# A decoder step on one core: 32 column diagonal tiles for the recurrence's levels, merged masked copies, and another order in sample attention

## The reference, cut to what matters

```python
rel = exp(b[t] - b[s]) for s <= t            # b: running sum of log f
att[t, s] = sum_k q[t, k] * rel[t, s, k] * k_[s, k]
o = att @ i + (q * exp(b)) @ state
```

```python
score = einsum('bqh,bqhs->bqs', wi, relu(qi . ki_all)) ; top_idx = top_k(score, 64)
logits = q . k_all[top_idx] * scale ; p = softmax(logits) ; o = p @ v_all[top_idx]
```

## Time and profile before

| | us |
|---|---|
| median of 3 runs (2674.17 to 2674.98) | 2674.17 |
| the profiled execution's own time | 2675.92 |
| its span, first to last instruction | 2674.1 |
| PE matmuls busy | 2607.7 |
| DVE, ACT, POOL busy | 915.5, 841.2, 1096.8 |

### The profile page before, as it was taken

One profiled execution on the slowest core, in us unless ns is written; L12 is line 12 of the kernel. 1 busy time (PEld: TensorE's weight loads), 2 busy tenths in 40 slices (PEclk: granted clock), 3 DMA queues, 4 the chain that ended last, 5 costly groups with the idle time before them and its releaser, 6 DMA issues. The chain is left out here.

```text
span 2674.1 us, 55031 instructions
## 1 busy us (share of the span) xinstructions
PE 2607.7 (98%) x22892; PEld 2484.1 (93%) x22892; DVE 915.5 (34%) x2323; ACT 841.2 (31%) x1359; POOL 1096.8 (41%) x886
## 2 busy tenths in 40 slices
PE   6999999999999999999999999999999999999998
PEld 4999998999988989999999999989998889899998
DVE  4111113267793441111131111134678824311111
ACT  2321222323464233222233222233244622331221
POOL 4444345333322454444554344542343326444443
PEclk9999999999999999999999999999999999999999
DMA  6434444312223434332633322641222234222322
GB/s 249 142 127 150 142 161 154 128 64 91 94 65 95 156 106 142 124 106 94 198 131 128 125 97 94 204 157 64 64 91 80 64 95 175 79 91 83 105 81 81
DMA packets 107060, 312.96 MB, mean 117 GB/s; under 512 B 18476, under 2 KB 45130, under 8 KB 89434
## 3 DMA queue, kind: packets, MB, share of 16 engines
q1 hardware_dynamic: 97952, 290.60, 32.0%
q10 hardware_dynamic: 8906, 19.44, 2.0%
HBM read 299.56 MB, written 10.66 MB: 116 GB/s over the span
## 5 line engine op out<-in xcount | busy, mean ns | idle before, releaser
L956 POOL TENSOR_TENSOR w_lo<-raw,w_hi 128x512 fp32r<-128x512 f32 (+1 forms) x800 | 1004.6, 1286 | 1543.1 <-ACT w_hi L1023 1535.3
L2186 PE MATMUL bank<-h_hi,w_hi 128*128 128x260 f32 x3744 | 1064.2, 284 | 2.8 <-ACT silu_g L1070 2.4
L2187 PE MATMUL bank<-h_hi,w_lo 128*128 128x260 f32 x3744 | 1053.0, 281 | 0.0
L2188 PE MATMUL bank<-h_lo,w_hi 128*128 128x260 f32 x3744 | 1052.7, 281 | 0.0
L2186 PEld LDWEIGHTS bank<-h_hi,w_hi 128*128 128x128 f32 x3744 | 702.5, 188 | 26.4 <-issue 23.9
L2187 PEld LDWEIGHTS bank<-h_hi,w_lo 128*128 128x128 f32 x3744 | 702.7, 188 | 0.0
L2188 PEld LDWEIGHTS bank<-h_lo,w_hi 128*128 128x128 f32 x3744 | 702.7, 188 | 0.0
L1023 ACT CAST w_hi<-raw 128x2048 fp32r<-128x2048 f32 (+3 forms) x219 | 376.5, 1719 | 478.6 <-PE bank L2188 375.8
L2186 PE MATMUL bank<-mid_hi,w_hi 128*128 128x260 f32 x1232 | 349.9, 284 | 0.0
L2188 PE MATMUL bank<-mid_lo,w_hi 128*128 128x260 f32 x1232 | 348.7, 283 | 0.0
L2187 PE MATMUL bank<-mid_hi,w_lo 128*128 128x260 f32 x1232 | 348.3, 283 | 0.0
(11 more groups left out here) (346 smaller groups left out, 3267.1 us busy)
## 6 DMA issues: line engine op xcount, KB each, us to landing
raw<-in_w SPq DMA_DIRECT2D x120, 1024.0 KB, 4.8
raw<-in_w SPq DMA_DIRECT2D x64, 512.0 KB, 4.5
raw<-in_w SPq DMA_DIRECT2D x32, 768.0 KB, 4.3
ada_ring<-in_ada SPq DMA_DIRECT2D x82, 256.0 KB, 5.2
raw<-in_w SPq DMA_DIRECT2D x32, 640.0 KB, 4.2
ada_ring<-in_ada SPq DMA_DIRECT2D x57, 320.0 KB, 5.3
ada_ring<-in_ada SPq DMA_DIRECT2D x57, 192.0 KB, 5.1
ada_low<-in_ada SPq DMA_DIRECT2D x20, 256.0 KB, 4.5
```

The source lines that it names most:

```text
L956: last = pool.tensor_tensor(w_lo[j][:, cols], raw[j][:, cols], w_hi[j][:, cols].bitcast(F32), ALU.subtract)
L2186: mm(out, wh(wb), xh(xb), start=(n == 0), stop=False)
L2187: mm(out, wl(wb), xh(xb), start=False, stop=False)
L2188: last = mm(out, wh(wb), xl(xb), start=False, stop=(n == len(blocks) - 1))
```

## The change

- `SAMPLE_FILLS` has ten places for nine. Group 31 goes from the place ahead of the key transposes to the one behind them; group 38 goes between the values and the transpose of the output; group 39 stays behind that transpose. ACT and PE follow the same table.
- DVE makes `own_diag` ahead of the reciprocal. The semaphore is renamed.
- The four masked copies of a level become one instruction over all chunks, with the mask broadcast over them.
- PE computes levels with 2h <= 32 (h = 1 to 16) as 32x32 tiles on the diagonal, four to a chunk. Level 0 stays whole, and 32 and 64 as they were. The rest of the bank isn't written; the masks don't take from it.

```diff
-SAMPLE_FILLS = ((27, 28), (29,), (30, 31), (32,), (33,), (34, 35), (36,), (37,), (38, 39))
+SAMPLE_FILLS = ((27, 28), (29,), (30,), (31, 32), (33,), (34, 35), (36,), (37,), (38,), (39,))
+TILE = 32
...
             # ACT, sample_attention
-                sample_fill(l, 7)
-                sample_fill(l, 8)
+                for place in (7, 8, 9):
+                    sample_fill(l, place)
...
             # DVE, hgrn: scores
-                    for c in range(TT):
-                        last = v.copy_predicated(
-                            att[:, c, :].rearrange("p (m a h) -> p m a h", a=2, h=h)[:, :, 1, :],
-                            masks[n].bitcast(U32),
-                            src[:, c * P:(c + 1) * P].rearrange("p (m a h) -> p m a h", a=2, h=h)[:, :, 1, :])
-                    last.then_inc(done, 1)
+                    v.copy_predicated(
+                        att[:].rearrange("p c (m a h) -> p c m a h", a=2, h=h)[:, :, :, 1, :],
+                        bc(masks[n].bitcast(U32).unsqueeze(1), [P, TT, m, h]),
+                        src[:, :].rearrange("p (c m a h) -> p c m a h", c=TT, a=2, h=h)[:, :, :, 1, :]).then_inc(done, 1)
...
             # DVE, sample_attention
+                v.tensor_scalar(own_diag[:], ident[0:NB * NH, 0:NB * NH], prob_s[:, PAST:LVIS], None, ALU.mult)\
+                 .then_inc(own_diag_ready, 1)
                 link(v.reciprocal(st_s[:, 3:4], st_s[:, 2:3]))
-                v.tensor_scalar(own_diag[:], ident[0:NB * NH, 0:NB * NH], prob_s[:, PAST:LVIS], None, ALU.mult)\
-                 .then_inc(own_scaled_probs, 1)
...
             # PE, hgrn
-                            if n < MASKED:
+                            if n == 0:
                                 last = mm(out[:, cs], hk[hd % 2][:, cs], qt[:, cs], start=True, stop=True)
+                                continue
+                            if 2 * h <= TILE:
+                                for s0 in range(0, P, TILE):
+                                    both = slice(c * P + s0, c * P + s0 + TILE)
+                                    last = mm(out[s0:s0 + TILE, both], hk[hd % 2][:, both], qt[:, both],
+                                              start=True, stop=True)
                                 continue
...
             # PE, sample_attention and merge
                 mm(out[0:NB * NH, 0:P], own_prob[:], vals[0:NB, TT, :], start=False, stop=True).then_inc(side_full, 1)
+                sample_fill(l, 8)
                 out = open_side(l, "s_oT")
...
             def merge(l):
-                sample_fill(l, 8)
+                sample_fill(l, 9)
```

More of the change, by code:

```diff
@@ L640, in build @@
         s_probs_ready = sem("s_probs_ready")
-        own_scaled_probs = sem("own_scaled_probs")
+        own_diag_ready = sem("own_diag_ready")
         blk_ready = sem("blk_ready")
@@ L2780, in sample_attention @@
                                         ident[0:NB * NH, 0:NB * NH])
-                pe.wait_ge(own_scaled_probs, l + 1)
+                pe.wait_ge(own_diag_ready, l + 1)
                 mm(out[0:NB, 2 * NB * NH:3 * NB * NH], gather_heads[:], own_diag[:], start=True, stop=True)\
```

## The result

Timed in turn with the kernel before (five runs each), the changed kernel takes 2660.38 us in the median (2658.65 to 2661.58) against 2674.17: ratio 0.9945, 95% interval 0.9932 to 0.9957. It is faster by 13.8 us between the medians, by 14.7 by the ratio. Forecast were 16.2 us, and 2658.0 us.

What follows compares the result with a forecast made beforehand. PE, busy 98% of the span, was taken as the bound. 12.4 + 0 + 3.0 + 0 + 0.8 = 16.2 us off the median of 2674.17 gave 2658.0 us, own range 2654 to 2662, or 2652 to 2667 with partial overlap and the clock.

Steps and rivals of the forecast that it cites:

- How a level costs PE: PE at the levels: 0.89 us for a wide level, 0.57 for h=32, of which 0.32 is the change of tile shape.
- part 1: Diagonal tiles on PE, h=1 to 16: four strips overlap, each of 40 levels saves 0.31 us, 12.4 us in all.
- The first rival: Levels on PE: tiles overlap only in part, 13.6 ns a start, 40 levels save 5.5 us, time 2664.9; chance 0.13.
- the floor: Rival at the cut levels: about 25 ns from start to start, 0.80 us for 32 starts, time 2679.5; chance 0.04.
- The stop before h=64: PE's stops there in heads 1 and 2: PE and DVE both move by about 0.6 us, so 0 saved.
- Part 2: Merged masked copies on DVE: 7 us of DVE time less over 40 levels, hidden from PE, so costed at nothing.
- Part 3: Key transposes: PE's 1.60 us stop for ACT's first key copy goes but for 0.1, 1.5 a layer, 3.0 us saved.
- Part 4: own_diag ahead of the reciprocal on DVE: starts 0.19 us earlier but meets the same POOL piece, so 0 saved.
- Part 5: Outputs of sample attention: gate group 38 covers PE's wait between s_o and its transpose, 0.8 us saved.
- The clock: Rival: layer 1's low clock over 1962 to 1970 falls otherwise; neither layer falling gives 2654.6 us, both 2661.4; chance 0.08.

Runs made afterwards that it cites:

- tiles_of_64: The changed kernel with levels h=1 to h=16 in two strips of 64 columns instead of four of 32; 2666.09 us in one run.
- strip_by_strip: The changed kernel with the same 16 matmuls of 32 columns a level, four of one strip behind each other; 2678.23 us in one run.
- tiles_alone: The kernel before with only the 32 column tiles for levels h=1 to h=16; 2661.28 us, ratio 0.9950.
- order_alone: The kernel before with only the new places of the gate groups, and so of key copies and outputs; 2674.93 us, ratio 1.000.
- rotary_later: The changed kernel with DVE's rotary step of level h=16 issued one level later; 2659.87 us in one run.
- level0_tiled: The changed kernel with level 0 cut into 32 column tiles too; 2670.61 us, ratio 0.9983.
- outputs_later: The changed kernel with level 0 tiled too and a head's outputs issued one token group later; 2652.76 us, ratio 0.9915.
- copies_alone: The kernel before with only the four masked copies of a level merged into one; 2677.34 us in one run.
- own_diag_alone: The kernel before with only own_diag put ahead of the reciprocal; 2674.49 us in one run.
- early_exp: The changed kernel with ACT's exponential ahead of the evacuations of gate groups 34, 35 and 36; 2655.31 us, ratio 0.9923.
- best: outputs_later with early_exp and rotary_later in one kernel; 2645.9 us, ratio 0.9889.

## Why the prediction was right

The forecast was 2658.0 us, and 2660.38 came out, within its own range of 2654 to 2662. The largest term is shown, in size and in mechanism. That the sum came so near is in part luck: the 3.8 us of parts 3 and 5 did not reach the time when they were tried alone, and a clock that was low for less time elsewhere and an earlier start, 2.1 us in the trace that the forecast did not count on, made up for much of that.

**How a level costs PE, and part 1 (12.4 us).** Right in every term. Marks 0.82 apart, 0.26 inside, the rest the change of tile shape: 40 levels x 0.31. The forecast took eight groups of four at the pace of the pairs of h=32, and that is what the starts show, one group every 32 ns. tiles_of_64 and strip_by_strip bear out the mechanism: strips side by side, at a pace that a tile's columns set. The first rival (32 starts in 0.435 us) and the floor (0.80) fall. The Trainium skill ("TensorE: Matmul & The Clock Gate", Part 1) has about 25 ns as the least from start to start: the runs show 8 ns on average over four strips and 32 ns only from one start to the next in the same strip, so its figure may stand for one strip, and not for the engine.

**The stop before h=64 (0).** The stops of heads 1 and 2 came out at about 0.5 us each, as before; in total there are 4.3 us instead of 4.0, since two small ones joined at h=32 of the last head. But this holds for tiles and copies together. tiles_alone shows 5.0.

**Part 2, merged copies (0).** The term that was mis-sized. "I cost it at nothing: DVE stands 0.86 us before the next level even in this crowded stretch" looks at the levels up to h=16. In the last two levels DVE is what PE waits for, and there the merged copy counts: 0.2 us a layer alone, about 0.4 beside the tiles. I had used the same 0.18 us for the stop before h=64 and so counted it there, as part of the chain that stays level; the sum is right and its split is not. Of the 12.4 us in the recurrence the tiles alone bring 11.6 and the merged copies beside them 0.8. The 7 us of DVE's own time were too many as well: at h=1 and h=2 nothing is saved, and DVE is busy 3.4 us less (915.5 against 912.1).

**Part 3, key copies (3.0).** Measured 3.3 in the stretch, 1.67 a layer in order_alone and in the whole change; I had left 0.1 a layer that was not needed, and 1.67 lies a little above my upper bound of 1.6.

**Part 4 (0).** Measured 0, and for the reason given: the time is POOL's piece, not the place in DVE's order. It takes 0.25 us when it is moved away from the piece.

**Part 5, outputs (0.8).** The 0.4 a layer is there where the clock stays up (13.44 against 13.84). It did not in the changed kernel, where the stretch is 1.1 to 1.2 us longer than before. Parts 3 and 5 together are order_alone, and its median is 0.5 us under the kernel before, where 3.8 were forecast.

**The clock.** By the two traces the change brought 15.5 us where 16.2 were forecast: the keys brought 0.3 more, the falls behind `own_diag` took 3.1, and the stretches at state_q, behind layer 0's norm and at the start of the kernel brought 2.1 together (1.6 - 1.1 + 1.6). I had weighed falls near state_q and none behind `own_diag`, so that the 3.1 and the 2.1 nearly cancel is luck. With the two stops ahead of it, the clock fell there in 12 of 16 places of kernels with the new order (all four in the two traces of the changed kernel, both in order_alone, rotary_later and tiles_of_64, none in strip_by_strip, one each in level0_tiled and outputs_later), and in 2 of 8 with the old order (before, tiles_alone, copies_alone, own_diag_alone). Where the stops are gone it fell in none of 4 (early_exp, best). So taking the stops away ended the falls there, and the new order comes with more of them; what in the order does it wasn't tried. Falls near state_q vary between executions of one program by up to 3.2 us, so no single trace settles the last 2 us, and how the medians' 13.8 splits below that stays open.

## What to carry to other kernels

A block-diagonal product on TensorE is worth cutting into one small tile for each 32 columns, issued so that neighbours stand in different column strips: for one level, four strips of 32 took 0.26 us from first to last start where two of 64 took 0.46 and the 128 wide tiles 0.78, and the same small tiles in strip order 0.70. To this comes the change of shape, 0.32 us with 32 columns. Pay for it only where PE does not stop right behind: a saved 0.6 us that lengthened a stop from 0.40 to 0.95 us was followed by a lower clock in five of six places and cost 10 us, and with the stop covered the kernel gained 7.5. Read merged or moved work on a hidden engine against the one place where PE waits for that engine, not against the places where it has slack.

## What the runs showed of the hardware

- fp32 matmuls with 32 columns of weights and 32 to stream, in four column strips, start 8 ns apart on average, 32 of them in 0.26 us. Entering and leaving costs 0.32 us in sum with tiles of 32 columns, whether 16 or 32 starts lie between and in either order, 0.35 with tiles of 64, and 0.11 around a level of 128 wide tiles. This fits the drain at a change of mode that the Trainium skill's page "TensorEngine Tiling (Array Packing)" has under Tiling Modes.
- Less work on PE can come out slower through the clock: level0_tiled needs less of PE's time at level 0 than the changed kernel (0.26 instead of 0.84 us), has a granted clock of 0.988 over its span against 0.994, and its two recurrences are 4.35 and 5.95 us longer.
- A DVE operation of 64 elements took 0.25 us away from POOL's pieces and 0.78 to 0.97 beside one; DVE's 256 element products took 0.42 and 1.51. POOL's four pieces took 4.97 and 6.02 to 6.64.
- One masked copy of 256 elements takes 0.34 us to the next start where four of 64 take 0.53 (levels h=4 to 16), but 0.54 either way at h=1 and h=2.
